# Transformer blocks on one core: the memory's keys and values projected around the attentions, and attention rows turned by halves

## The chip, the core and the metric

The kernel runs on one NeuronCore of a Trainium2 chip, as one launch. The metric is the device time of that launch in microseconds (us), as a median of several runs. TensorE (PE) multiplies, VectorE (DVE) and ScalarE (ACT) copy, split and reduce, GpSimd (POOL) does the small roots of the norms, and SyncE (SP) only issues the loads of weights. Each engine runs its own instructions in the order in which they are written. They meet through semaphores.

## What is computed

Three transformer layers on 256 rows of width 1024, in float32. The first has a masked attention of 8 heads beside a retention of 4 heads, then a cross attention of 4 heads onto 256 memory rows, then a gated MLP:

```python
h = rms_norm(x, g_pre_mix[l]);  proj = h @ w_in[l]
...
mo = merge_heads(moba_attention(mq, mk, split_heads(mv, MOBA_HEADS)))
ro = retention(rq, rk, split_heads(rv, RET_HEADS))
ro = ro * lax.rsqrt(jnp.mean(ro * ro, axis=-1, keepdims=True) + NORM_EPS)
ro = jax.nn.silu(rg) * merge_heads(ro).astype(x.dtype)
x = x + rms_norm(jnp.concatenate([mo, ro], axis=-1) @ w_out[l], g_post_mix[l])
h = rms_norm(x, g_pre_cross[l]);  mem_n = rms_norm(mem, g_mem[l])
x = x + rms_norm(cross_attention(h, mem_n, w_cq[l], w_ckv[l], w_co[l]), g_post_cross[l])
h = rms_norm(x, g_pre_ffn[l]);  gu = h @ w_gate_up[l]
x = x + rms_norm((jax.nn.silu(gu[..., :D_FF]) * gu[..., D_FF:]) @ w_down[l], g_post_ffn[l])
```

With 256 rows there is one block of keys, so `moba_attention` is a plain causal attention. The second layer has an indexed sparse attention (`dsa`) and a short convolution, the third a latent attention of 16 heads (`mla`). Each of these two ends in a squared-ReLU MLP (`mlp0`, `mlp1`).

## The kernel before

**Tiling.** The 256 rows are two tiles of 128 tokens, `t` = 0 and 1. A weight matrix comes in *units* of up to 1 MB (`SCHEDULE` lists all of them). A projection of 1024 by 1024 is four units `j` = 0 to 3 of two blocks `k` of 128 rows each, with outputs 1024 wide in two PSUM banks. Four units can be held at a time (`RING`).

**Three products.** Precision comes from splitting. ScalarE writes the rounded high part `w_hi` of a unit (`split`, L572), then VectorE the rest `w_lo` (L950, or L952 where the gain of a norm is folded in). The rows are split in the same way: TensorE turns four blocks of 128 columns into a PSUM bank (`turn`, L1463), ScalarE copies the high part `hT_hi` out (L591), VectorE subtracts it to get `hT_lo` (L967), and only then is the bank free (`tb_free`). `products` (L1398) then issues, for each `k`, high rows by `w_hi`, high rows by `w_lo`, low rows by `w_hi`, each for both banks: 12 matmuls for a unit and a token tile, 24 for a unit. Before the first of them TensorE waits for `w_low` of the unit (`split_ready`). A unit's slot is given back (`w_used`) when its last product with tile 1 is issued.

**Projections.** `project` runs all units for tile 0, then all for tile 1. Its `hooks` put other work of TensorE ahead of a given `(t, j)`. When a tile is through, ScalarE copies it out of PSUM (`group`, L631, "eviction"), and adds to `acc_copied`; TensorE waits for it before it writes those banks again.

**Attention.** For each head `hd`, TensorE makes scores (L1498), turns the probabilities of head `hd - 2` (L1506) and multiplies the values of head `hd - 3` (L1515). VectorE makes the masked maximum (L1096, or L1100 in the cross attention) and copies the turned probabilities (L1109). ScalarE makes the exponentials (L725). At the end VectorE waits for the last head, takes the reciprocal of all sums and scales the output into `h` (`normalise`, L1122 and L1124). Only then TensorE turns `h`, and the output projection follows.

**Order of the first layer.** Input projection, first attention, retention, `out`; then the memory's keys (`mem_k`), the memory's values (`mem_v`), the cross queries (`cross_q`), the cross attention, `cross_o`, and the MLP `ffn`. The memory's rows are turned into `gT_hi` and `gT_lo` near the end of the input projection. `SCHEDULE`, the loads on SyncE, and the code of ScalarE, VectorE and TensorE all carry this order, written out by hand.

**Boundaries.** After an output projection, `boundary` weighs the result by a gain (`weigh`, L1030, from PSUM into `h`), adds it to the stream `x` (`add_to_stream`, L1039), splits the next units in between, and turns the new rows. ScalarE takes the sum of squares of each tile (L645), GpSimd the root (L463, L464). An MLP that follows starts with its chunk 0. Its first hidden tile (`part`, L745 and L747 on ScalarE, `act_part`, L1134 and L1138 on VectorE) comes after `split_to(m.u0 + 3)`, the split of the fourth unit. TensorE waits for that hidden tile before it starts chunk 1, since the PSUM bank is used again.

## Time and profile before

| | us |
|---|---|
| median of 3 runs | 1106.6 |
| lowest, highest | 1105.09, 1107.01 |
| the profiled execution, its own time | 1103.71 |
| its span, first to last instruction | 1101.9 |
| TensorE busy | 1048.6 (95%) |
| VectorE busy | 656.2 (60%) |
| ScalarE busy | 563.5 (51%) |

A profile is of one execution, so durations read from it add up to its own span. The profile has a page with busy times and the costliest groups, a timeline (each instruction with its start, its duration and the idle time before it, with what ended that), the chain of work that ended last, and tables of stretches with the granted TensorE clock. Ends of matmuls are modelled: in a run of 512-wide matmuls each is drawn as 0.39 us long while the next starts 0.23 us after it, so that the drawn idle time after such a matmul is 0.16 us less than what TensorE lost.

### The profile page before, as it was taken

To read this page: it belongs to the slowest core of one execution; us is meant where nothing else is said; L and a number is where in the kernel's file an instruction comes from. 1 tells how busy PE (TensorE), PEld (TensorE's weight loads), DVE (VectorE), ACT (ScalarE), POOL (GpSimd) and SP (SyncE) were. 2 spreads that over 40 slices of the span, in tenths; PEclk is the share of its full clock that TensorE was granted. 3 is DMA by queue.
4 is the path that set the end of the run, shared out by engine and by line. 5 is a ranking of instruction groups with operands and counts; after the bars stand their busy time and mean duration, and the time that the engine had idled before them with its cause. 6 is when DMAs were issued, how large, how long until landed. Compare 5 with 4: busy or idle time off the path is not lost.

```text
span 1101.9 us, 13842 instructions
## 1 busy us (share of the span) xinstructions
PE 1048.6 (95%) x5080; PEld 872.6 (79%) x5080; DVE 656.2 (60%) x1010; ACT 563.5 (51%) x855; POOL 97.7 (9%) x127
## 2 busy tenths in 40 slices
PE   7998999999999999999989999999997999999997
PEld 6887788777888888878767788888886877888886
DVE  5567654466645655648786655555654866555553
ACT  6555554346554544744454654544454646545441
POOL 2010110001000000203540100000140001000000
PEclk9999999999999999999999999999999999999999
DMA  9642265224455455543422555554252225555521
GB/s 345 274 177 77 94 233 189 77 78 170 172 188 211 157 188 200 211 153 115 153 77 106 219 191 181 199 190 145 75 182 110 77 107 199 191 180 200 188 80 38
DMA packets 28461, 176.29 MB, mean 160 GB/s; under 512 B 3248, under 2 KB 3392, under 8 KB 9984
## 3 DMA queue, kind: packets, MB, share of 16 engines
q1 hardware_dynamic: 26784, 170.08, 42.6%
q0 software_dynamic: 1456, 5.48, 1.3%
q8 instruction: 29, 0.48, 0.2%
q10 hardware_dynamic: 176, 0.13, 0.0%
q14 instruction: 16, 0.13, 0.0%
HBM read 174.62 MB, written 1.05 MB: 159 GB/s over the span
## 4 chain that ended last, share of the span: by engine, by line
PE 84%; DVE 7%; ACT 4%; issue 2%; POOL 2%; DMA 1%; SPq 0%; DVEq 0%; ACTq 0%; POOLq 0%
PE PS L1398 74%; PE PS L1463 4%; DVE w_lo L952 2%; PE PS L1515 2%; ACT w_hi L572 2%; PE PS L1593 2%; PE PS L1498 2%; DVE work L1096 1%; POOL rstd L464 1%; POOL h L487 1%; DMA x<-in_x 1%; DVE w_lo L950 1%; PE PS L1506 1%; DVE h L1281 1%; POOL arena L480 1%
## 5 line engine op out<-in xcount | busy, mean ns | idle before, releaser
L952 DVE SCALAR_TENSOR_TENSOR w_lo<-w_raw,gcol,w_hi 128x512 fp32r<-128x512 f32 (+4 forms) x322 | 269.5, 894 | 206.0 <-ACT w_hi L572 205.4
L1398 PE MATMUL PS<-w_hi,hT_hi 128*128 128x512 f32 (+3 forms) x904 | 320.1, 395 | 17.8 <-DVE hT_lo L967 5.1
L1398 PE MATMUL PS<-w_lo,hT_hi 128*128 128x512 f32 (+3 forms) x904 | 313.2, 388 | 0.0
L1398 PE MATMUL PS<-w_hi,hT_lo 128*128 128x512 f32 (+3 forms) x904 | 313.0, 387 | 0.0
L572 ACT ACTIVATE w_hi<-w_raw,gcol 128x512 fp32r<-128x512 f32 (+4 forms) x322 | 243.4, 823 | 99.9 <-PE PS L1398 99.2
L1398 PEld LDWEIGHTS PS<-w_hi,hT_hi 128*128 128x128 f32 x904 | 168.3, 190 | 53.3 <-DVE w_lo L952 11.7
L1398 PEld LDWEIGHTS PS<-w_hi,hT_lo 128*128 128x128 f32 x904 | 170.7, 190 | 34.0
L1398 PEld LDWEIGHTS PS<-w_lo,hT_hi 128*128 128x128 f32 x904 | 170.8, 190 | 32.8
L950 DVE TENSOR_TENSOR w_lo<-w_raw,w_hi 128x2048 fp32r<-128x2048 f32 (+1 forms) x70 | 135.8, 1953 | 89.3 <-ACT w_hi L572 89.2
L572 ACT ACTIVATE w_hi<-w_raw 128x2048 fp32r<-128x2048 f32 (+1 forms) x70 | 114.8, 1645 | 102.8 <-PE PS L1398 102.8
L1398 PE MATMUL PS<-w_hi,gT_hi 128*128 128x512 f32 x408 | 126.2, 390 | 0.0
L1398 PE MATMUL PS<-w_hi,gT_lo 128*128 128x512 f32 x408 | 125.8, 390 | 0.0
L1398 PE MATMUL PS<-w_lo,gT_hi 128*128 128x512 f32 x408 | 125.7, 389 | 0.0
L1398 PEld LDWEIGHTS PS<-w_lo,gT_hi 128*128 128x128 f32 x408 | 76.6, 188 | 16.0
L1398 PEld LDWEIGHTS PS<-w_hi,gT_lo 128*128 128x128 f32 x408 | 76.5, 188 | 15.9
L463 POOL TENSOR_SCALAR msq<-ssq 128x1 f32<-128x1 f32 (+1 forms) x31 | 11.0, 354 | 872.9 <-ACT work L645 827.5
L1398 PEld LDWEIGHTS PS<-w_hi,gT_hi 128*128 128x128 f32 x408 | 76.1, 188 | 15.4
L631 ACT ACTIVATE arena<-PS,rstd 128x1024 f32<-128x1024 f32 (+1 forms) x24 | 25.0, 1043 | 60.6 <-PE PS L1398 44.7
L591 ACT ACTIVATE hT_hi<-PS 128x512 fp32r<-128x512 f32 (+1 forms) x46 | 25.2, 582 | 53.5 <-PE PS L1463 53.4
L967 DVE TENSOR_TENSOR hT_lo<-PS,hT_hi 128x512 fp32r<-128x512 f32 (+1 forms) x46 | 29.2, 668 | 30.2 <-ACT hT_hi L591 30.0
L1498 PE MATMUL PS<-arena 128*128 128x256 f32 (+1 forms) x160 | 36.4, 361 | 6.8 <-ACT arena L631 2.7
L645 ACT ACTIVATE work<-PS 128x1024 f32<-128x1024 f32 x14 | 14.4, 1028 | 51.7 <-PE PS L1398 51.7
(149 smaller groups left out, 790.5 us busy)
## 6 DMA issues: line engine op xcount, KB each, us to landing
w_raw<-in_w SPq DMA_DIRECT2D x64, 1024.0 KB, 4.8
w_raw<-in_w_gu SPq DMA_DIRECT2D x22, 1024.0 KB, 4.8
w_raw<-in_w_in SPq DMA_DIRECT2D x11, 1024.0 KB, 7.3
w_raw<-in_w_dn SPq DMA_DIRECT2D x22, 512.0 KB, 5.2
w_raw<-in_w_out SPq DMA_DIRECT2D x4, 1024.0 KB, 4.8
w_raw<-in_w_mem_k SPq DMA_DIRECT2D x4, 1024.0 KB, 4.8
w_raw<-in_w_mem_v SPq DMA_DIRECT2D x4, 1024.0 KB, 4.9
w_raw<-in_w_cq SPq DMA_DIRECT2D x4, 1024.0 KB, 5.7
```

Source lines behind the costliest of these rows:

```text
L572: ins = act.activation(w_hi[:, u % RING, k * w:(k + 1) * w], w_raw[:, u % RAW, k * w:(k + 1) * w], ACT.Copy, scale=1.0 if col is None else ...
L591: act.activation(d, PS[:, 4 + n["tb"] % 4, 0:blocks * P].rearrange("p (b m) -> p b m", m=P), ACT.Copy).then_inc(tb_high, 1)
L631: ins = act.activation(dst, src, ACT.Copy, scale=scale)
L645: act.activation(square_out if out is None else out, src, ACT.Square, scale=scale, accum_out=ssq[:, n["norm"]:n["norm"] + 1]).then_inc(ss_ ...
L950: ins = dve.tensor_tensor(lo, raw, hi, ALU.subtract)
L952: ins = dve.scalar_tensor_tensor(out=lo, in0=raw, scalar=gcol[:, col + TURNED * k:col + TURNED * k + 1], in1=hi, op0=ALU.mult, op1=ALU.sub ...
L967: dve.tensor_tensor(lo, PS[:, 4 + n["tb"] % 4, 0:blocks * P].rearrange("p (b m) -> p b m", m=P), hi.bitcast(F32), ALU.subtract).then_inc(t ...
L1398: mm = pe.matmul(bank(t, j)[:, 0:width], rows[:, kc0 + k, tok], w[:, s, at:at + width], start=begin and i == 0, stop=end and i == 2)
L1463: mm = pe.transpose(PS[0:rows, 4 + n["tb"] % 4, i * P:(i + 1) * P], src, ident[:])
L1498: mm = pe.matmul(PS[:, 4 + hd % 2, c0:c1], q, k, start=i == 0, stop=i == len(pairs) - 1)
L1515: mm = pe.matmul(out_banks(a, t)[:, hd * a.dv:(hd + 1) * a.dv], a.ET[hd % 2][:, c0 + s * P:c0 + (s + 1) * P], a.v(hd, s), start=s == 0, st ...
L1593: mm = pe.transpose(m.turn_bank[t][:, b * P:(b + 1) * P], hidden[:, t, b * P:(b + 1) * P], ident[:])
```

## The change

In the first layer `mem_k` is projected straight after the input projection, unit by unit for both tiles, with the scores of attention heads 0 and 1 ahead of its last unit's two halves. `mem_v` is projected behind `cross_q` in the same way, with the scores of the first two cross heads inside it. The loads and splits follow that order. `products` goes through a unit in three passes (high by high, low rows by `w_hi`, high rows by `w_lo`) and waits for `w_high` first and for `w_low` only ahead of the third. The output of the cross attention and of `mla` is scaled, turned and split in two halves of 512 columns, the first half while the last heads still run; `cross_o` and `odd_out` start on it. `weigh` writes into `work`. The retention's scaling and gate are one instruction a head instead of two a tile. At the start of each MLP the first hidden tile comes ahead of the split of the fourth unit.

```diff
-            ("out", plain_units(4)), ("mem_k", gained("mem", 4, 2, 2048)), ("mem_v", gained("mem", 4, 2, 2048)),
-            ("cross_q", gained("pre_cross", 4, 2, 2048)), ("cross_o", plain_units(4)),
+            ("mem_k", gained("mem", 4, 2, 2048)), ("out", plain_units(4)), ("cross_q", gained("pre_cross", 4, 2, 2048)),
+            ("mem_v", gained("mem", 4, 2, 2048)), ("cross_o", plain_units(4)),
...
+        cross.score_bank, cross.prob_bank = 6, 4
...
 # ScalarE, boundary
                 if not hidden_next:
                     high_rows(hT_hi, 1)
-                split_to(e + 3)
+                    split_to(e + 3)
...
 # ScalarE, mlp (VectorE the same with act_part)
-                split_to(m.u0 + 3)
                 part(0, tiles=[0])
+                split_to(m.u0 + 3)
+                part(0, tiles=[1])
                 split_to(m.u0 + 4)
-                part(0, tiles=[1])
...
 # ScalarE, memory keys and first attention
+            n["used"] += 4
+            split_to(n["used"] + 1)
+            attention(moba, [0])
+            split_to(n["used"] + 2)
+            evict(0, rows2(k_tok), mem_rows)
+            attention(moba, [1])
+            evict(1, rows2(k_tok), mem_rows)
+            attention(moba, range(2, moba.H), False)
+            split_to(n["used"] + 3)
...
 # VectorE, the same place
+            split_to(n["used"] + 1)
+            attention(moba, [0])
+            split_to(n["used"] + 2)
+            attention(moba, range(1, moba.H + 2), False)
...
 # VectorE, attention
+                    elif rows is not None:
+                        normalise_half(a, rows, hd - a.H, 0)
                     if hd >= 2:
                         copy_turned(hd - 2)
+            def normalise_half(a, dst, t, half):
+                heads = slice(half * a.H // 2, (half + 1) * a.H // 2)
+                if t == 0:
+                    dve.wait_ge(a.summed, heads.stop)
+                    steps.link(dve.reciprocal(a.sums[:, heads, :], a.sums[:, heads, :]))
...
 # TensorE, products
-                for k in range(kcs):
-                    begin, end = first and k == 0, last and k == kcs - 1
-                    for i, (rows, w) in enumerate(((hi, w_hi), (hi, w_lo), (lo, w_hi))):
+                if fresh:
+                    high_ready(u, it)
+                for i, (rows, w) in enumerate(((hi, w_hi), (lo, w_hi), (hi, w_lo))):
+                    if fresh and i == 2:
+                        split_ready(u, it)
+                    for k in range(kcs):
...
+            def out_project(tile, **more):
+                at = n["tb"] - 2
+                project(4, 2, wide, rows=lambda t, half: at + 2 * half + t, second=lambda: pe.wait_ge(h_ready, n["h"] + 1),
+                        hooks={(0, 1): lambda: turn_half(tile, 512), (1, 2): tile0}, **more)
...
 # TensorE, the first layer
-            copied()
-            turned(6)
-            attention(moba)
+            by_unit = [(t, j) for j in range(4) for t in range(TT)]
+            project(4, 2, wide, gT_hi, gT_lo, copies=2, rows=n["tb"] - 6, order=by_unit,
+                    hooks={(0, 3): moba_scores, (1, 3): lambda: attention(moba, [1])})
+            attention(moba, [2])
+            copied()
+            attention(moba, range(3, moba.H + 3))
...
-            project(4, 2, wide, gT_hi, gT_lo, copies=2, hooks={(1, 0): tile1})
-            project(4, 2, wide, gT_hi, gT_lo, copies=2, hooks={(1, 1): lambda: turn_rows(k_tok, False)})
-            project(4, 2, wide, copies=2)
-            copied()
-            turn_rows(q_tok, False)
-            turned(4)
-            attention(cross)
-            turn_rows(h)
-            rows = n["tb"] - 4
-            project(4, 2, wide, rows=rows, hooks={(1, 2): tile0})
-            mlp(ffn, within=half_of(0, 0))
+            project(4, 2, wide, copies=2, rows=n["tb"] - 2, hooks={(0, 3): tile1})
+            project(4, 2, wide, gT_hi, gT_lo, copies=2, order=by_unit,
+                    hooks={(0, 1): query_rows, (0, 3): cross_scores, (1, 3): lambda: attention(cross, [1])})
+            attention(cross, [2])
+            copied()
+            attention(cross, range(3, cross.H + 3), h)
+            out_project(h)
+            mlp(ffn, between={(2, 0): half_of(0, 0)})
```

**VectorE around the first two heads of the first attention.** Before, the two maxima of a head (the rows with `causal`) follow each other head by head:

```order
L950 TENSOR_TENSOR w_lo<-w_raw,w_hi 128x2048 x2
L1096 ISA work,attention_max<-PS,causal 128x128
L1096 ISA attention_max 128x1
L1096 ISA work,attention_max<-PS,causal 128x256
L1096 ISA attention_max 128x1
L1103 TENSOR_SCALAR attention_bias<-attention_max 128x2
L1096 ISA work,attention_max<-PS,causal 128x128
```

After (L981 is the old L950, L1127 the old L1096, L1134 the old L1103):

```order
L981 TENSOR_TENSOR w_lo<-w_raw,w_hi 128x2048 x2
L1127 ISA work,attention_max<-PS,causal 128x128
L1127 ISA attention_max 128x1
L1127 ISA work,attention_max<-PS,causal 128x256
L1127 ISA attention_max 128x1
L1134 TENSOR_SCALAR attention_bias<-attention_max 128x2
L981 TENSOR_TENSOR w_lo<-w_raw,w_hi 128x2048
L1127 ISA work,attention_max<-PS,causal 128x128
```

The third unit of `out` is now split between head 0 and head 1.

**VectorE from the second tile's rows to the first hidden tiles of `ffn`.** Before:

```order
L1039 SCALAR_TENSOR_TENSOR x<-h,rstd,x 128x512 x2
L967 TENSOR_TENSOR hT_lo<-PS,hT_hi 128x4x128 x2
L952 SCALAR_TENSOR_TENSOR w_lo<-w_raw,gcol,w_hi 128x512 x8
L1134 SCALAR_TENSOR_TENSOR arena<-PS,rstd,arena 128x256
L950 TENSOR_TENSOR w_lo<-w_raw,w_hi 128x1024
```

After:

```order
L1070 SCALAR_TENSOR_TENSOR x<-work,rstd,x 128x512 x2
L998 TENSOR_TENSOR hT_lo<-PS,hT_hi 128x4x128 x2
L983 SCALAR_TENSOR_TENSOR w_lo<-w_raw,gcol,w_hi 128x512 x4
L1186 SCALAR_TENSOR_TENSOR arena<-PS,rstd,arena 128x256
L983 SCALAR_TENSOR_TENSOR w_lo<-w_raw,gcol,w_hi 128x512 x4
```

The first hidden tile (L1134, now L1186) stands between the third and the fourth unit instead of behind both.

**VectorE in the last heads of the cross attention, after.** Here L1140 is the copy of the turned probabilities (before L1109), and L1157 and L1158 are the reciprocal and the scaling of one half:

```order
L1140 COPY work<-PS 128x512
L1157 RECIPROCAL attention_sum<-attention_sum 128x4
L1158 TENSOR_TENSOR h<-PS,attention_sum 128x512
L1140 COPY work<-PS 128x512
L1158 TENSOR_TENSOR h<-PS,attention_sum 128x512
```

Before, the reciprocal and two scalings of 128x1024 stood behind all four copies. Now the first half's reciprocal stands ahead of the copy for head 2.

## Rows read from the trace of the kernel before

**Rows 1.** Page, part 1: busy us (share of the span), instructions.

```profile
PE 1048.6 (95%) x5080; PEld 872.6 (79%) x5080; DVE 656.2 (60%) x1010; ACT 563.5 (51%) x855; POOL 97.7 (9%) x127
```

**Rows 2.** Chain that ended last: start us, us, what (engine, tile, line, instructions).

```profile
88.37 0.99 ACT work L725 x4
...
92.27 0.33 PE PS L1506 x3
92.59 0.62 PE PS L1515 x6
93.21 0.71 PE PS L1498 x4
...
97.27 0.29 DVE work L1096
...
98.03 0.57 DVE work L1109
...
101.39 1.36 PE PS L1532 x8
...
213.64 1.73 PE PS L1498 x8
...
367.20 16.38 PE PS L1398 x72
```

**Rows 3.** Timeline where the first attention starts: start, us, what, [idle before, releaser].

```profile
84.74 3.81 PE L1498 MATMUL PS<-arena 128*128 128x128 f32 x12 [2.70 <-ACT arena L631]
...
83.55 1.13 ACT L631 ACTIVATE arena<-PS,rstd 128x1024 f32<-128x1024 f32 x1
```

**Rows 4.** Chain from the retention's norm to the third unit of `out`.

```profile
112.21 1.30 DVE h L1243 x2
...
116.07 1.91 ACT w_hi L572
...
118.00 2.30 DVE w_lo L950
...
120.35 8.50 PE PS L1398 x36
```

**Rows 5.** Timeline of TensorE: cross queries turned, cross attention's rows turned.

```profile
204.36 1.97 PE L1463 MATMUL PS<-ident,arena 128*128 128x128 f32 x16 [1.21 <-ACT arena L631]
...
225.15 2.22 PE L1463 MATMUL PS<-ident,h 128*128 128x128 f32 x16 [1.56 <-DVE h L1124]
```

**Rows 6.** Timeline where `ffn` starts its chunk 1, all engines.

```profile
257.50 0.94 POOL L464 TENSOR_TENSOR rstd<-msq,neg_half 128x1 f32<-128x1 f32 x1
...
260.74 1.28 ACT L745 ACT_TABLE_LOAD   x1
262.04 0.47 ACT L745 ACTIVATE arena<-PS,rstd 128x256 f32<-128x256 f32 x1
...
260.76 2.74 DVE L952 SCALAR_TENSOR_TENSOR w_lo<-w_raw,gcol,w_hi 128x512 fp32r<-128x512 f32 x4 [1.40 <-ACT w_hi L572]
263.41 0.48 DVE L1134 SCALAR_TENSOR_TENSOR arena<-PS,rstd,arena 128x256 f32<-128x256 f32 x1
...
264.04 0.47 PE L1398 MATMUL PS<-w_hi,hT_hi 128*128 128x512 f32 x1 [1.86 <-DVE arena L1134]
```

**Rows 7.** Timeline of TensorE where `mlp0` starts its chunk 1.

```profile
620.05 0.52 PE L1398 MATMUL PS<-w_hi,hT_hi 128*128 128x512 f32 x1 [2.06 <-DVE arena L1138]
```

**Rows 8.** Stretches: length, busy us (instructions), granted clock as a share, DMA.

```profile
265.30:268.80 3.50, 3.50 (x10) 2.76 (x9) 1.25 (x2) 0.00 (x0) 0.00 (x0) 0.51 0.92 320
...
470.00:473.50 3.50, 3.50 (x12) 2.92 (x12) 3.42 (x8) 2.74 (x5) 0.00 (x0) 0.52 0.90 332
```

**Rows 9.** Timeline of TensorE at a unit of the second layer's `conv` projection.

```profile
533.89 0.74 PE L1398 MATMUL PS<-w_hi,hT_hi 128*128 128x512 f32 x2 [1.04 <-DVE w_lo L952]
```

**Rows 10.** Timeline at `ukv` in the third layer: VectorE, then TensorE.

```profile
828.00 4.87 DVE L952 SCALAR_TENSOR_TENSOR w_lo<-w_raw,gcol,w_hi 128x1024 fp32r<-128x1024 f32 x4 [1.18 <-ACT w_hi L572]
...
835.06 1.20 PE L1463 MATMUL PS<-ident,h 128*96 128x128 f32 x8 [0.19 <-DVE h L1017]
```

277 lines of the change are left out of this document (160 added, 117 removed).

## The prediction

> **What bounds the kernel now.** I read the page's busy times first. TensorE is busy 95% of the span, VectorE 60% [rows 1]. The chain of work then shows long pieces of products that follow without a gap, 72 in 16.38 us, or 0.2275 us each [rows 2]. The change leaves the number and shape of the products as they are, so nearly all of the 1102 us stays. What can go is time in which TensorE waits, and time at the lower clock. So I went through TensorE's timeline for rows with idle time, and for each I ask whether the change puts work there and what comes late next. To a drawn idle time after products 0.16 us is added, since a product is drawn longer (0.39) than its distance to the next. Positive numbers below are time saved.
>
> **Start of the first attention.** The products of the input projection could have gone on at 84.74 - 2.70 - 0.16 = 81.88 [rows 3]; the attention is through at 101.39 [rows 2]: 19.5 us. A head costs TensorE 0.33 + 0.62 + 0.71 = 1.66 us [rows 2], eight cost 13.3. So 6.2 us are waits for evictions and first exponentials, and slow clock. Now the keys' four units stand there, 24 x 0.2275 = 5.46 us each. Count from their start. The scores of head 0 come after three units (16.4 to 17.1), half a unit follows to 19.8, scores of head 1 to 20.5, half a unit to 23.3, then scores and turning, 1.0 us, to 24.3. There TensorE waits for the second eviction of the keys. Who leads to it: maximum of head 0 (0.8, from 97.27 to 98.03) to 17.9, exponentials (1.0) to 18.9 [rows 2], ScalarE's split of the third `out` unit (1.9) to 20.8, VectorE's part of it (2.3) to 23.1 [rows 4], maximum and exponentials of head 1 to 24.9, eviction (1.1) [rows 3] to 26.0. That is 1.7 us, and with semaphores about 2.1 us late. Behind the waiting TensorE instruction stand all values of the attention. The gain is 6.2 - 2.1 = 4.1; I take 3.8, for a slower end of the last heads. Ends: 6.2 if nothing is late, 2 if the new wait also brings the low clock.
>
> **`out`.** The gated rows depend on VectorE's scaling, which starts at 112.21, while the chain goes on over a split of the third unit (1.91, 2.30) to 120.35 [rows 4]. Now 16 turnings of the keys (16 x 0.11 = 1.75 us, the same as elsewhere before) fill part of that wait, and that unit has been split earlier. Eight 128x128 instructions replace four of 128x512 on VectorE; the nearest row is the 128x128 maximum of 0.29 us [rows 2], so the first tile costs 1.2 instead of 2.0. But VectorE now has its split of the last unit (2.3) directly ahead. I take 1.3, ends 0.5 and 2.3.
>
> **Start of the cross attention.** From 204.36 - 1.21 - 0.16 = 203.0 to 225.15 - 1.56 - 0.15 = 223.4 [rows 5] are 20.4 us. The work is 16 turnings (1.75), 4 x 1.73 for scores, 4 x 1.73 for values [rows 2] and four turnings of a head at 0.44 (four of 0.11): 17.4. The 3.0 us of waits now lie behind the values' units. Here the second eviction comes in time: from the scores of head 0, the path is 1.7 + 0.9 + 1.0 + 1.9 + 2.3 + 0.9 + 1.0 + 1.1 = 10.8 us, and TensorE reaches it after 1.7 + 2.7 + 1.7 + 2.7 + 1.7 + 0.4 = 10.9. Gain 3.0, ends 2 and 3.0.
>
> **Its end.** From 223.4 to 227.4 [rows 5] TensorE does 1.75 us of turnings, 2.2 are lost. By halves the reciprocal and first scaling fall into the last heads. But VectorE waits for the values of head 1 ahead of its copy for head 2, and TensorE's values of head 2 are queued behind that copy: 0.2 + 0.65 + 0.7 for the three, less 0.44 of turning, gives 1.2 us of new wait. Gain 1.0, ends 0 and 2.2. In `mla`, where the same two turnings cost the same 2.2, the first eight heads are long done when VectorE asks, so only some 0.6 is left: 1.6.
>
> **MLP starts.** `ffn` stands still for 1.86 + 0.16 = 2.0 us for its first hidden tile [rows 6]; the two others for 2.2 each, one row for both [rows 7]. The root is there at 257.50 + 0.94 = 258.44. Table load 1.28 and activation 0.47 then give about 260.0, VectorE's 0.48 gives 260.5, ahead of TensorE's 262.0. What is late next is the second hidden tile, behind the fourth unit's splits: ScalarE 2.6 us to 262.5, VectorE 2.74 to 265.3, then 0.48 [rows 6], while TensorE wants it at 262.0 + 12 x 0.2275 = 264.8. So 1.0 is left of 2.0. In the other two there is no table load, and 0.3 is left of 2.2. Gain 1.0 + 1.9 + 1.9 = 4.8, ends 3 and 6.4.
>
> **The clock.** Right behind the wait in `ffn`, TensorE is granted 0.51, its 1.2 GHz level, for about 3.4 us [rows 8], which costs products 1.7 us. The same stands behind both other MLP starts, and in each case TensorE had stood idle for 2.0 us or more. One fall, at 470, came without idle time [rows 8], while it issued 80-column products, and stays. With waits of 1.0 us and less I take these three falls away: 3 x 1.7 = 5.1, ends 0 and 5.1.
>
> **The passes.** A wait for `w_lo` now comes 8 products (1.8 us) later in a unit with two blocks. At `conv` this takes the 1.04 + 0.16 of the row [rows 9], and another 0.8 in its next unit, down to 0.2: 1.8. Unit waits at `uq` (0.7) and twice at `out` projections (0.4 here, the other is counted) follow the pattern: 1.1. At `ukv` it saves nothing: VectorE's splits run from 828.00 to 832.9, its rotation after them, and TensorE must wait for that until 835.06 [rows 10]. It will get there 1.8 us earlier and stand idle for 3.6 us, so the low clock falls on work behind it instead of before: -1.6. The added waits and the pace of products: the loads of stationary rows are one for each product, as before (5080 and 5080, [rows 1]), so I take 0, ends 0 and -25 (a rival).
>
> **Sum.** 3.8 + 1.3 + 3.0 + 1.0 + 1.6 + 4.8 + 5.1 + 1.8 + 1.1 - 1.6 = 21.9. The profiled execution took 1103.7 and would take 1081.8; the median of the runs lies 2.9 higher, 1106.6 - 21.9 = 1084.7.
>
> **A rule against it.** ScalarE's change of function costs 1.28 us in the row, and the activation starts 0.02 us after it (260.74 + 1.28, next 262.04) [rows 6]. The Trainium skill, "ScalarE: Activation LUTs", section "What ACT_TABLE_LOAD costs", says 1.28 us and a drain of 1.38 beside it, 2.66 in all, for every switch. The trace doesn't agree, as no such drain is drawn between these two rows. By that rule the load in `ffn` would lead to a second hidden tile 1.4 us later.
>
> **Rivals.** (a) *The low clock stays, or comes back elsewhere* (at the keys' new wait of 2 us, at the MLP starts): the moved waits add up to enough idle time for it. For it speaks the fall at 470 without idle; against it that TensorE passed waits of 1.7 us at 225.15 at full clock. Price 5.1 + 1.3: 1091. (b) *The drain*: if a table load holds ScalarE 1.4 us longer, `ffn` keeps a wait of 2.4 and its low clock: 1.4 + 1.7, 1088. (c) *New waits eat the moved starts*: the order on ScalarE and VectorE between head 0 and head 1 delays the attentions by more than I count, both starts and both ends give nothing (9.4): 1094. (d) *Slower than before*: products in the new order have another pace. The third pass uses `w_lo` against rows last loaded a pass ago, and each unit has a second wait. There are some 3,700 products of 512 columns. From 6 ns more on each (0.2275 to 0.2335) it costs 22 us and eats the whole gain; 10 ns give 1122. Against it: pairs of products on the same rows (wide outputs) and single ones (512) run at the same 0.2275, waits that are met cost nothing in the loops. (e) *The change doesn't do what it says*, since the halves of `mem_k` are bound by the loads: its units' slots come free 5.5 us apart, SyncE is far ahead; nothing speaks for it, time as (c).
>
> **Chances.** Forecast 0.62; (a) 0.15, (b) 0.04, (c) and (e) 0.14, (d) 0.05, of which 0.03 slower. The forecast's own spread, from the ends above, is 1078 to 1090. The range takes in (a), (b) and most of (c): 1077 to 1095. A measurement can tell 0.2%, about 2 us. Faster 0.95, within it 0.02, slower 0.03.
>
> **What would show it.** Right: products at 0.2275 us; about 2 us of idle before the values of head 0; no idle row ahead of the second cross head; at most 1.0 us at the three MLP starts and full clock behind them; 3.6 us of idle at `ukv`. Wrong: a pace above 0.23, a wait of over 1 us at the first product of `cross_q` (rows of the stream not ready), low-clock stretches at as many places as before, or VectorE behind in the keys' units.

## The result, and the profile after

The changed kernel takes 1089.9 us (median of 4, 1089.14 to 1090.19), the kernel before beside it 1106.3 us (1105.09 to 1107.01): ratio 0.9852, 95% interval 0.9841 to 0.9864. That is 16.4 us less, where 21.9 were forecast. The profiled execution after took 1089.14 us with a span of 1087.3. TensorE's busy time hardly moved, as should be, since its instructions are the same [rows 1]:

```profile
span 1087.3 us, 13860 instructions
## 1 busy us (share of the span) xinstructions
PE 1044.9 (96%) x5080; PEld 872.4 (80%) x5080; DVE 655.1 (60%) x1020; ACT 564.1 (52%) x855; POOL 99.8 (9%) x127
```

**Where the time went.** Both kernels have 5080 products, so the k-th product can be looked up in each trace. The table gives the time between the starts of two of them, the first being product 0. Between 351 and 1060 the change moves products, so of the kernel before and `b_mlp` on the one side and all others on the other only the sum of the two rows can be compared there (150.3 us before, 142.6 after). Elsewhere the same product is at most a dozen places further on. The kernels of the experiments are explained below.

| TensorE's products, stage | before | b_mlp | after | after_again | a_front | a_bias2 | best | best_front |
|---|---|---|---|---|---|---|---|---|
| 0 to 351, input projection | 75.5 | 75.3 | 76.3 | 76.6 | 76.3 | 77.0 | 76.0 | 76.4 |
| to 560, first attention (before: to the middle of `out`) | 41.6 | 42.5 | 39.1 | 40.8 | 39.1 | 40.8 | 37.8 | 37.8 |
| to 1060, the rest up to `cross_o` | 108.7 | 108.7 | 103.5 | 103.5 | 103.5 | 103.5 | 101.4 | 101.4 |
| to 1216, rest of `cross_o`, start of `ffn` | 37.4 | 35.0 | 35.0 | 35.0 | 35.1 | 35.1 | 35.0 | 35.0 |
| to 2430 | 262.4 | 262.4 | 262.4 | 264.0 | 262.4 | 264.0 | 262.4 | 262.4 |
| to 2541, end of `conv` | 24.9 | 24.9 | 23.1 | 23.1 | 24.9 | 23.1 | 23.1 | 24.9 |
| to 2700, `dsa` attention, start of `even_out` | 35.1 | 35.1 | **38.4** | 35.8 | 35.0 | 33.5 | 32.8 | 31.2 |
| to 3740, rest of `even_out`, `mlp0`, `down`, `uq`'s first tile | 222.1 | 218.7 | 218.0 | 217.9 | 218.6 | 217.9 | 217.9 | 218.7 |
| to 3815, rest of `uq` | 13.6 | 13.6 | 14.0 | 13.9 | 13.6 | 14.0 | 14.9 | 13.6 |
| to 3900, `ukv` | 21.5 | 21.4 | 22.8 | 22.8 | 21.4 | 23.9 | 19.5 | 19.8 |
| 4000 to 5079, `mla`'s end, `odd_out`, `mlp1` | 228.3 | 226.0 | 224.0 | 224.0 | 227.5 | 224.0 | 223.8 | 227.3 |

(3900 to 4000 is 17.9 in all.) From before to after that is a gain of 14.6 us of the 1089.0 between the first and the last product. Of the stages that were forecast faster the rest of `uq` is 0.4 slower, and 3.4 us are lost in the row of `dsa`, which the prediction did not mention. One thing was plain only with several executions: the stretches at the 1.2 GHz level don't lie at the same products each time. The changed kernel's own second trace (after_again) has one in the first attention, where the first has none, and less of them in `dsa`. A difference of 1.7 us in one stage of one trace can be this alone, and in `dsa` the changed kernel's two traces differ by 2.6.

**What came as forecast.** The keys' new wait, with the split ahead of head 1's maximum, as the path in the prediction has it (1.75 us idle, 2.0 between starts):

```profile
103.53 2.29 DVE L981 TENSOR_TENSOR w_lo<-w_raw,w_hi 128x2048 fp32r<-128x2048 f32 x1 [2.86 <-ACT w_hi L572]
...
107.51 1.09 ACT L631 ACTIVATE h<-PS,rstd 128x1024 f32<-128x1024 f32 x1
...
106.42 0.49 PE L1580 MATMUL PS<-ident,work 128*128 128x128 f32 x3
108.65 0.92 PE L1572 MATMUL PS<-arena 128*128 128x128 f32 x4 [1.75 <-ACT h L631]
```

The cross attention starts without a wait [rows 5] and has the forecast one at its end (first row below, where L1140 stands behind one half's scaling). The second hidden tile is what is late in `ffn` (1.07 + 0.16 us for 2.0 [rows 6]), and the two other starts have 0.21 + 0.16 for 2.2 each, one row for both [rows 7]:

```profile
215.16 1.13 PE L1589 MATMUL PS<-arena,work 128*128 128x256 f32 x4 [1.16 <-DVE work L1140]
...
259.04 1.20 PE L1468 MATMUL PS<-w_hi,hT_hi 128*128 128x512 f32 x4 [1.07 <-DVE arena L1186]
...
613.08 1.20 PE L1468 MATMUL PS<-w_hi,hT_hi 128*128 128x512 f32 x4 [0.21 <-DVE arena L1190]
...
528.21 1.21 PE L1468 MATMUL PS<-w_lo,hT_hi 128*128 128x512 f32 x4 [0.17 <-DVE w_lo L983]
...
823.51 3.32 PE L1537 MATMUL PS<-ident,h 128*96 128x128 f32 x16 [3.33 <-DVE h L1048]
```

The last two rows are `conv`'s remaining wait for `w_lo` (1.04 before [rows 9]; 0.2 forecast) and the idle time at `ukv` (3.3 idle, 3.7 from one start to the next; 3.6 forecast).

The clock, in stretches (columns: from:to, length, busy and instructions of each engine, granted clock, DMA share, GB/s): full speed behind the starts of `mlp0` and `mlp1`, still half speed at 461, as at 470 before [rows 8], at `ukv`, and now around `dsa`:

```profile
461.20:464.60 3.40, 3.40 (x9) 2.64 (x9) 3.37 (x8) 2.76 (x5) 0.00 (x0) 0.51 0.93 354
549.90:553.30 3.40, 2.90 (x8) 2.02 (x8) 1.56 (x6) 0.89 (x1) 2.87 (x2) 0.50 0.54 227
556.80:563.60 6.80, 6.67 (x26) 5.70 (x27) 5.74 (x18) 3.29 (x15) 6.16 (x3) 0.51 0.00 0
823.00:826.40 3.40, 2.89 (x14) 2.76 (x15) 1.14 (x3) 0.66 (x2) 0.00 (x0) 0.51 0.76 306
612.00:620.00 8.00, 7.79 (x38) 6.19 (x37) 6.62 (x6) 5.91 (x8) 0.00 (x0) 1.00 0.92 335
912.00:920.00 8.00, 7.79 (x39) 6.22 (x38) 6.49 (x7) 5.91 (x9) 0.00 (x0) 1.00 0.79 294
```

**What did not.** At `out`, GpSimd's mean of squares for 8 columns took 2.17 us; before it took 0.20:

```profile
129.04 2.28 DVE L981 TENSOR_TENSOR w_lo<-w_raw,w_hi 128x2048 fp32r<-128x2048 f32 x1
133.15 2.16 DVE L1304 SCALAR_TENSOR_TENSOR arena<-PS,rstd,arena 128x128 f32<-128x128 f32 x8 [1.82 <-POOL rstd L464]
...
129.21 2.17 POOL L463 TENSOR_SCALAR msq<-ssq 128x8 f32<-128x8 f32 x1 [62.90 <-DVE ssq L1296]
131.46 1.65 POOL L464 TENSOR_TENSOR rstd<-msq,neg_half 128x8 f32<-128x8 f32 x1
```

The same instruction in the kernel before:

```profile
110.25 0.20 POOL L463 TENSOR_SCALAR msq<-ssq 128x8 f32<-128x8 f32 x1 [44.68 <-DVE ssq L1236]
```

The prediction saw VectorE's split of the last unit ahead of the scaling, but counted it on VectorE alone. It also stands in GpSimd's way: it ends at 131.32, GpSimd's instruction at 131.38.

At `dsa`, TensorE waits 2.39 us for VectorE's product L1386 (1.06 before), then for the biases of the heads:

```profile
548.20 1.26 PE L1537 MATMUL PS<-ident,arena 128*128 128x128 f32 x8 [2.39 <-DVE arena L1386]
...
554.31 0.92 PE L1572 MATMUL PS<-arena 128*128 128x128 f32 x4 [1.08 <-DVE attention_bias L1134]
...
545.25 2.29 DVE L981 TENSOR_TENSOR w_lo<-w_raw,w_hi 128x2048 fp32r<-128x2048 f32 x1
547.46 1.29 DVE L1386 TENSOR_TENSOR arena<-arena 128x512 f32<-128x512 f32 x2
...
552.66 1.59 DVE L1134 TENSOR_SCALAR attention_bias<-attention_max 128x2 f32<-128x2 f32 x1
...
554.83 1.85 DVE L1134 TENSOR_SCALAR attention_bias<-attention_max 128x2 f32<-128x2 f32 x1
...
565.21 0.17 DVE L1134 TENSOR_SCALAR attention_bias<-attention_max 128x2 f32<-128x2 f32 x1
...
552.33 1.89 POOL L502 TENSOR_TENSOR arena<-arena,conv_w 128x1020 f32<-128x1020 f32 x1
554.30 2.35 POOL L503 TENSOR_TENSOR arena<-arena 128x1020 f32<-128x1020 f32 x1
```

Two things are to be seen. First, VectorE's chain (splits, top-k, split, copies, split, product) bounds this place. Its top-k part began 9.34 us earlier than before (530.95 for 540.29), while TensorE came 11.2 us earlier, so that of the 1.8 us gained in `conv` 1.3 are idle time at this product. Second, a bias of 2 columns takes 0.17 us when GpSimd is idle and up to 1.85 while it convolves, and it ends with GpSimd's instruction (552.66 + 1.59 = 554.25, GpSimd 554.22; 554.83 + 1.85 = 556.68, GpSimd 556.65). In the kernel before the same rows stand, but the first bias met only the last 0.3 us of a GpSimd instruction (until 562.08):

```profile
561.76 0.34 DVE L1103 TENSOR_SCALAR attention_bias<-attention_max 128x2 f32<-128x2 f32 x1
...
562.68 1.39 DVE L1103 TENSOR_SCALAR attention_bias<-attention_max 128x2 f32<-128x2 f32 x1
...
560.18 1.90 POOL L500 TENSOR_TENSOR arena<-arena,conv_w 128x1024 f32<-128x1024 f32 x1 [20.12 <-DVE arena L985]
```

So the cost was there before. What the change altered is how the engines meet. Summed over the whole row of `dsa`, though, TensorE's drawn idle time grew only from 7.2 to 7.6 us, since longer waits at some products made others shorter. The rest of the 3.4 us is products at half speed: none before, 10.2 us of the row after, 3.4 us in after_again (where 0.8 us are lost).

### The profile page after: what moved, and what is told of

The parts are those of the page before. It is cut to its first block, busy times and chain, and to the rows that moved or that the text cites. A ratio compares the mean times of both kernels' runs of the same rounds, so it can differ in the third digit from the quotient of the medians.

```text
span 1087.3 us, 13860 instructions
## 1 busy us (share of the span) xinstructions
PE 1044.9 (96%) x5080; PEld 872.4 (80%) x5080; DVE 655.1 (60%) x1020; ACT 564.1 (52%) x855; POOL 99.8 (9%) x127
## 3 DMA queue, kind: packets, MB, share of 16 engines
HBM read 174.62 MB, written 1.05 MB: 162 GB/s over the span
## 4 chain that ended last, share of the span: by engine, by line
PE 82%; DVE 9%; ACT 3%; issue 3%; POOL 2%; DMA 1%; SPq 0%; DVEq 0%; ACTq 0%; POOLq 0%
PE PS L1468 71%; PE PS L1537 3%; DVE w_lo L983 3%; PE PS L1589 2%; PE PS L1572 2%; ACT w_hi L572 2%; PE PS L1679 2%; DVE w_lo L981 1%; DMA x<-in_x 1%; DVE work L1127 1%; POOL h L487 1%; PE PS L1580 1%; DVE h L1347 1%; POOL arena L480 1%; ACT work L653 0%
## 5 line engine op out<-in xcount | busy, mean ns | idle before, releaser
L1468 PE MATMUL PS<-w_hi,hT_hi 128*128 128x512 f32 (+3 forms) x904 | 246.4, 393 | 7.8 <-DVE hT_lo L998 3.0
L1468 PE MATMUL PS<-w_hi,hT_lo 128*128 128x512 f32 (+3 forms) x904 | 240.2, 386 | 0.0
L1468 PE MATMUL PS<-w_lo,hT_hi 128*128 128x512 f32 (+3 forms) x904 | 238.9, 385 | 0.9 <-DVE w_lo L983 0.8
L1468 PEld LDWEIGHTS PS<-w_lo,hT_hi 128*128 128x128 f32 x904 | 167.5, 188 | 35.9 <-DVE w_lo L983 2.4
L1468 PEld LDWEIGHTS PS<-w_hi,hT_hi 128*128 128x128 f32 x904 | 164.0, 189 | 40.1 <-issue 3.8
L1468 PEld LDWEIGHTS PS<-w_hi,hT_lo 128*128 128x128 f32 x904 | 168.1, 189 | 33.2
L981 DVE TENSOR_TENSOR w_lo<-w_raw,w_hi 128x2048 fp32r<-128x2048 f32 (+1 forms) x70 | 135.7, 1954 | 83.7 <-ACT w_hi L572 83.6
L1468 PE MATMUL PS<-w_hi,gT_hi 128*128 128x512 f32 x408 | 113.9, 392 | 0.0
L1468 PE MATMUL PS<-w_lo,gT_hi 128*128 128x512 f32 x408 | 112.9, 390 | 0.0
L1468 PE MATMUL PS<-w_hi,gT_lo 128*128 128x512 f32 x408 | 112.7, 389 | 0.0
L1468 PEld LDWEIGHTS PS<-w_hi,gT_lo 128*128 128x128 f32 x408 | 76.6, 188 | 16.0
L631 ACT ACTIVATE arena<-PS,rstd 128x1024 f32<-128x1024 f32 (+1 forms) x22 | 22.8, 1036 | 44.7 <-PE PS L1468 30.7
L733 ACT ACTIVATE work<-work,attention_bias 128x128 f32<-128x128 f32 x64 | 28.5, 446 | 31.2 <-DVE attention_bias L1134 31.2
```

What stands on the lines that cost most here:

```text
L631: ins = act.activation(dst, src, ACT.Copy, scale=scale)
L733: ins = act.activation(a.E[hd % 3][:, c0:c1], src, ACT.Exp, bias=a.nb[:, hd, t:t + 1], scale=a.scale, accum_out=a.sums[:, hd, t:t + 1])
L981: ins = dve.tensor_tensor(lo, raw, hi, ALU.subtract)
L1468: mm = pe.matmul(bank(t, j)[:, 0:width], rows[:, kc0 + k, tok], w[:, s, at:at + width], start=begin and i == 0, stop=end and i == 2)
```

## The experiments

My theory of the shortfall was then: GpSimd blocked at `out` (1 to 2 us), VectorE's chain, the blocked biases and the clock at `dsa` (3.4), and small terms. Rivals were the new order of the passes, the keys' wait and the end of cross. Each run is timed beside the kernel before (medians of 1105.15 to 1106.15 us in four groups).

**The MLP starts alone** (b_mlp, the kernel before with this part only; here ScalarE's part of the edit; VectorE's moves the same steps):

```diff
                 if not hidden_next:
                     high_rows(hT_hi, 1)
-                split_to(e + 3)
+                    split_to(e + 3)
...
-                split_to(m.u0 + 3)
                 part(0, tiles=[0])
+                split_to(m.u0 + 3)
+                part(0, tiles=[1])
                 split_to(m.u0 + 4)
-                part(0, tiles=[1])
```

> The kernel before with one part of the change alone: at the three MLP starts ScalarE and VectorE serve the first hidden tile between the splits of the third and fourth unit, and ScalarE's boundary split stands where the change has it. Theory (the prediction's own terms): waits 1.0 + 1.9 + 1.9 less and three stretches at the 1.2 GHz level gone, 5.1, together 9.9 us, so about 1096.4 us; full clock behind all three MLP starts, and nothing moved elsewhere. Rival: the clock's gain needs the other parts too (other idle times go, or the low clock moves elsewhere): then only the waits, 4.8 us, 1101.5.

Measured 1098.9 us (ratio 0.9942, 0.9926 to 0.9958), its executions in two groups, 1096.2 to 1097.5 (granted clock 0.992 and 0.993) and 1100.3 to 1100.5 (0.986). The median lies between the two cases, and the lower group at the theory's 1096.4; the trace is of that group, so what the upper one has more is not shown. At the places themselves the theory's 9.9 is met to 0.6: 2.4 at `ffn`, 3.5 at `mlp0` and 3.4 at `mlp1` (between products 4280 and 4340), and the clock behind them is full:

```profile
265.00:270.00 5.00, 3.94 (x20) 2.89 (x19) 3.96 (x5) 0.79 (x1) 0.00 (x0) 1.00 0.62 229
620.00:626.00 6.00, 6.00 (x33) 5.01 (x32) 4.83 (x4) 3.91 (x7) 0.00 (x0) 1.00 0.91 360
878.80:882.10 3.30, 3.20 (x15) 3.20 (x16) 2.43 (x4) 1.54 (x3) 0.00 (x0) 0.50 0.00 0
```

But a stretch of half speed now stands at `odd_out` (last row), where the kernel before has idle time at full clock. It costs 1.1 us (products 4120 to 4200). The one near the first attention has moved from 84 to 117.6. Part of what an MLP start gives back in clock is taken elsewhere.

**The late wait for `w_lo`** (a_front, the changed kernel without it):

```diff
                 if fresh:
-                    high_ready(u, it)
+                    split_ready(u, it)
                 for i, (rows, w) in enumerate(((hi, w_hi), (lo, w_hi), (hi, w_lo))):
-                    if fresh and i == 2:
-                        split_ready(u, it)
```

> The changed kernel with the wait for w_lo put back ahead of each unit's first product (the order of the three passes stays). The prediction's ledger says it is worth 1.8 at conv and 1.1 elsewhere, less 1.6 lost at ukv: without it 1089.9 + 1.3 = 1091.2 us. Theory from the trace of after: the conv gain is given back a few us later, because VectorE's own chain (splits, top-k, split, copies, split, product) bounds the start of the dsa attention: TensorE's wait of 2.39 us there falls to about 1.0, and the 3.3 us at ukv to about 1.6 us. Then 1088 to 1090 us, so that the later wait is worth nothing here or costs a little.

Measured 1090.4 us (0.9869, 0.9851 to 0.9886): between the two, and the intervals of this and the changed kernel overlap. The table tells more than the sum. `conv` loses 1.8, and `dsa` gets 3.4 back (0.8 against after_again), with TensorE's wait down to 1.06 as the theory has it. `uq` gets 0.4 back and loses 0.7 in its first tile. `ukv` gets 1.35 back, but not as the theory has it: the wait of 3.33 is down to 1.45, yet one of 2.82 for `w_lo` stands ahead of it (817.81), and the idle time of the stage is 0.3 longer; what is gained is the half-speed stretch, which is gone. What neither case had is the last stage, which loses 3.4:

```profile
548.75 1.26 PE L1535 MATMUL PS<-ident,arena 128*128 128x128 f32 x8 [1.06 <-DVE arena L1386]
...
879.78 1.16 PE L1466 MATMUL PS<-w_hi,hT_hi 128*128 128x512 f32 x4 [2.23 <-DVE w_lo L981]
...
877.34 4.49 DVE L981 TENSOR_TENSOR w_lo<-w_raw,w_hi 128x2048 fp32r<-128x2048 f32 x2 [1.00 <-ACT w_hi L572]
```

By halves, `odd_out`'s products start before VectorE has split their unit. In the changed kernel the split starts as late (879.93), but is wanted only in the third pass and costs 0.18 us. So the late wait carries the halves of `mla`.

The totals show what the two waits trade. TensorE's drawn idle time is 34.1 us here and 29.7 in the changed kernel, but the half-speed stretches between the first and the last product sum to 6.8 us here and to 17.1 there. The late wait saves idle time and pays for most of it in clock.

**GpSimd at `out`** (a_pool):

```diff
-            split_to(n["used"] + 3)
             dve.wait_ge(ret_rstd, 1)
             dve.wait_ge(gate_ready, 1)
...
             low_banks(2, half_rows(4))
+            split_to(n["used"] + 3)
             boundary(0, 4, hidden_next=False)
```

> The changed kernel with VectorE's split of out's last unit moved behind the gating and the low halves. Theory: GpSimd's tensor_scalar of 8 columns took 2.17 us at 129.21 because it stood locked out while VectorE's split ran (129.04 to 131.32); with VectorE idle it took 0.20 in the kernel before. Expected 0.2 us again, gating 2.0 us earlier, TensorE's two waits ahead of out (1.34 and 1.73 between starts) 2 us shorter in sum, 1088 us. Rival: the 2.17 us is how GpSimd's span happens to be drawn, or the gating waits for something else (ScalarE's reading of the gate): then the row stays near 2, or the gating stays at 133.15 and the time at 1089.9.

Measured 1086.7 us (0.9840, 0.9823 to 0.9856). The theory holds; the lock is seen by its absence:

```profile
128.67 0.20 POOL L463 TENSOR_SCALAR msq<-ssq 128x8 f32<-128x8 f32 x1 [62.90 <-DVE ssq L1296]
...
130.63 2.16 DVE L1303 SCALAR_TENSOR_TENSOR arena<-PS,rstd,arena 128x128 f32<-128x128 f32 x8 [2.06 <-POOL rstd L464]
...
136.36 1.17 PE L1468 MATMUL PS<-w_hi,hT_hi 128*128 128x512 f32 x4 [1.62 <-DVE hT_lo L998]
```

The gating starts 2.5 us earlier, of which 0.5 comes from ahead of it, as the input projection is shorter in this trace. Products 560 to 1060 take 102.3 for 103.5: 1.2 us, not 2, since TensorE now waits (1.62) for VectorE's low part of the last turned rows, where it had two waits of 1.07 and 1.46. The medians differ by 3.2, more than this place gives; this trace has no half-speed stretch near 461, which is worth 1.6 us, and its executions spread from 1086.3 to 1089.5.

**VectorE's chain at `dsa`** (a_dsa: `after_group(4, lambda: plain_banks(4, turned_qk3), 1)` with 0 for 1, so that one split comes in the middle of the heads):

> The changed kernel with VectorE's split of one even_out unit moved from ahead of the two products for the convolution rows to the middle of the dsa attention. Theory: VectorE's chain bounds the start of this attention, so TensorE's wait of 2.39 us at 548.20 falls by about 2.2, and with less idle time the stretch at the low clock behind it may go as well: gain 1.5 to 4 us, 1086 to 1088.4, less what the 2.3 us cost in the middle of the heads (up to 1). Rival: TensorE waits there for ScalarE's evictions or the turned rows, so that the wait stays: 1089.9, or the split in the middle of the heads costs 2.3 us: 1090.

Measured 1092.1 us (0.9879, 0.9863 to 0.9895), slower than the changed kernel by 2.2, where 1.5 to 4 us less were expected. The first step goes the expected way, but less far: the wait at L1386 falls from 2.39 to 1.05, by 1.34 for 2.2. The gain is lost behind it, and more: the stage takes 40.8 us. The rival (1090) was right in kind and too low in price.

```profile
546.67 1.26 PE L1537 MATMUL PS<-ident,arena 128*128 128x128 f32 x8 [1.05 <-DVE arena L1386]
...
564.03 1.54 PE L1589 MATMUL PS<-arena,work 128*128 128x64 f32 x6 [4.49 <-DVE work L1140]
...
557.48 3.81 DVE L981 TENSOR_TENSOR w_lo<-w_raw,w_hi 128x2048 fp32r<-128x2048 f32 x1
...
561.88 1.64 DVE L1134 TENSOR_SCALAR attention_bias<-attention_max 128x2 f32<-128x2 f32 x1
...
557.16 1.98 POOL L503 TENSOR_TENSOR arena<-arena 128x1016 f32<-128x1016 f32 x1
559.22 4.27 POOL L504 TENSOR_TENSOR arena<-arena 128x1024 f32<-128x1024 f32 x1
```

This is the lock from both sides. The split (2.29 alone) starts inside a GpSimd instruction, waits for its end (559.14) and ends 2.15 us later. GpSimd's last product (2.36 elsewhere) waits for the split in turn, and the next bias waits for that product.

**The bias without the lock** (a_bias2: in `dsa`, VectorE counts up `maxed` when the maxima are there, and ScalarE scales them):

```diff
+                    if a is dsa:
+                        act.activation(a.nb[:, hd, :], a.mx[:, hd, :], ACT.Copy, scale=-a.scale).then_inc(biased, 1)
+                        act.wait_ge(biased, hd + 1)
...
-                    dve.tensor_scalar(a.nb[:, hd, :], a.mx[:, hd, :], -a.scale, None, ALU.mult).then_inc(a.maxed, 1)
+                    if a is dsa:
+                        dve.sem_inc(a.maxed, 1)
+                    else:
+                        dve.tensor_scalar(a.nb[:, hd, :], a.mx[:, hd, :], -a.scale, None, ALU.mult).then_inc(a.maxed, 1)
```

> The changed kernel, but in the dsa attention ScalarE instead of VectorE scales the row maxima to the bias (2 columns a head), so that VectorE has only instructions that read PSUM while GpSimd convolves. Theory: VectorE's bias instruction took 1.59, 1.85, 1.38 and 1.02 us there, each ending within 0.05 us of the end of a GpSimd instruction of the convolution, against 0.17 us behind it: it is locked out. TensorE's scores wait for it. Expected: no such instruction, heads 0 to 4 at 1.7 us instead of 2.1 to 2.4, one or both stretches at the 1.2 GHz level (549.92 and 556.75) shorter or gone, 1 to 4 us gained: 1086 to 1089. Rival: VectorE's maxima take the lock's place (they read a mask from SBUF too and grow from 0.29 and 0.42), or ScalarE's extra instruction a head makes ScalarE the bound: 1089.9 or more.

Measured 1087.9 us (0.9831, 0.9811 to 0.9850). The stage takes 33.5 us, 5.0 less than in the changed kernel's first trace and 2.4 less than in its second. The second is the fair comparison, since it has as much low clock in this stage (3.4 us). VectorE's maxima keep 0.29 and 0.42 us, so the rival is out, and from head 4 on the heads follow at 1.65 us. The first bias had a price of its own: ScalarE's table load now stood behind the first bias, in the path.

```profile
556.38 0.20 ACT L730 ACTIVATE attention_bias<-attention_max 128x2 f32<-128x2 f32 x1 [2.81 <-DVEq L1139]
556.60 1.28 ACT L737 ACT_TABLE_LOAD   x1
```

**The keys' wait, two ways.** a_keys2 moves the split of the third `out` unit behind head 2, on ScalarE and VectorE:

```diff
             attention(moba, [0])
-            split_to(n["used"] + 2)
             evict(0, rows2(k_tok), mem_rows)
             attention(moba, [1])
             evict(1, rows2(k_tok), mem_rows)
-            attention(moba, range(2, moba.H), False)
+            attention(moba, [2], False)
+            split_to(n["used"] + 2)
+            attention(moba, range(3, moba.H), False)
```

> The changed kernel with the split of the third out unit moved on ScalarE and VectorE behind the work for head 2 of the first attention. Theory: that split (1.9 on ScalarE, 2.3 on VectorE) stands in the chain that leads to the second eviction of the keys and so to TensorE's wait of 2.0 us at 108.65; without it the wait is gone: 1088 us. Rival: the wait returns behind it, as the split is then late for out's third unit or lengthens a later head: 1089.9.

Measured 1095.7 us (0.9904, 0.9888 to 0.9920), 6 us slower than the changed kernel: the wait at the keys is gone (0.22), and one of 3.85 us stands two heads on, behind the same split, with 6.8 us at half speed from 111.2 on. The first attention takes 44.2 us for 39.1, 5.1 of the 5.8 us between the medians. The rival was right in kind and far too low in price.

```profile
106.02 0.92 PE L1573 MATMUL PS<-arena 128*128 128x128 f32 x4 [0.22 <-ACT h L631]
...
112.78 1.54 PE L1590 MATMUL PS<-arena,work 128*128 128x64 f32 x6 [3.85 <-DVE work L1141]
```

a_evict leaves the split and puts the second eviction ahead of head 1's exponentials, on ScalarE alone:

```diff
-            attention(moba, [1])
             evict(1, rows2(k_tok), mem_rows)
+            attention(moba, [1])
```

> The changed kernel with two steps of ScalarE exchanged in the first attention: the second eviction of the keys ahead of head 1's exponentials. The last product of the keys started at 105.55 in the trace of after, ScalarE was idle from 104.5 to 106.61, and evicted at 107.51, behind the exponentials of head 1, which wait for VectorE's split and maximum. Theory: the eviction starts at about 106.0, TensorE's wait at 108.65 falls from 1.75 to 0.3, exponentials of head 1 end at 108.0 instead of 107.5, ahead of their turning: 1.3 us gained, 1088.3. Rival: TensorE waits there for VectorE (maximum or copy of head 1), so the wait stays; or, as with the split moved behind head 2, it only comes later: 1089.5 or more.

Measured 1088.9 us (0.9845, 0.9831 to 0.9858), and the stage takes 37.8 for 39.1: 1.35 us, as forecast. The eviction starts at 105.61, in time that ScalarE had idle. The median shows 1.0 of it. The trace has a half-speed stretch from 136.3, in a wait of 1.46 us that the changed kernel has too, and loses 1.5 us behind it.

```profile
105.61 1.11 ACT L631 ACTIVATE h<-PS,rstd 128x1024 f32<-128x1024 f32 x1 [1.46 <-PE PS L1468]
...
106.78 0.92 PE L1572 MATMUL PS<-arena 128*128 128x128 f32 x4 [0.22 <-ACT h L631]
```

**The end of cross** (a_cross2: in each step `copy_turned` ahead of `normalise_half`):

> The changed kernel with VectorE's copy of the turned probabilities ahead of the first half of the scaling in every step of the last two. Theory: the wait of 1.2 us between the turning of the last head and the values at 215.16 is this order's cost: it goes, and the second tile's halves come 0.7 later at most, so 0.5 to 1.2 us gained at the end of cross and up to 0.6 in mla: 1089.0. Rival: the first rows are what TensorE waits for next, so that the same time is lost there: 1089.9.

Measured 1089.5 us (0.9841, 0.9820 to 0.9861), within what the changed kernel's executions spread. In the trace the wait at 215.16 is gone and products 920 to 1060 take 27.9 for 28.8 us, the last stage 0.15 less. 1 us is below what the medians resolve here, so this rests on the trace, and on best, which has the same 27.9. This trace, too, has a half-speed stretch at product 648 (from 138.8) that the changed kernel's has not, and loses 1.5 us there.

**The rotation at `ukv`** (a_ukv2):

```diff
-            after_group(3, lambda: queries_turned(0), 1)
+            after_group(3, lambda: queries_turned(0), 0)
             rotate(heads_of(stages[1], 96), 64, 16, cos4, sin4).then_inc(h_ready, 1)
+            split_to(n["used"] + 1)
```

> The changed kernel with VectorE's rotation of the second queries ahead of its split of the second ukv unit. Theory: the rotation ends 2 us earlier (about 821.5), TensorE's wait at 823.51 falls from 3.3 to 1.5 us, and the low clock behind it (822.99 to 826.40) may go: 1.8 to 3.5 us gained, 1086.4 to 1088.1, with a wait for w_lo in the second unit of at most 0.5. Rival: the rotation waits for ScalarE's reading of the queries (818.39 to 819.28 and 820.21 to 821.5), so that only 0.5 us is gained and the split is late for its unit: 1090.

Measured 1088.1 us (0.9846, 0.9831 to 0.9862). In the trace TensorE's wait is 1.41 us and the clock behind it full; the stage takes 19.5 for 22.8, 3.3 us, as the theory has it. The medians show 1.8 of it, within their spread.

`ukv` takes 22.7 to 24.2 us in the other kernels that leave its order alone and keep the late wait.

```profile
820.42 2.47 DVE L983 SCALAR_TENSOR_TENSOR w_lo<-w_raw,gcol,w_hi 128x1024 fp32r<-128x1024 f32 x2
820.56 1.95 PE L1538 MATMUL PS<-ident,h 128*96 128x128 f32 x16 [1.41 <-DVE h L1048]
```

**All that helped, together, and the changed kernel once more.**

> The changed kernel itself, beside the two others of this call on one chip, to see how much its executions spread and where its low-clock stretches lie in another one. Theory: 1089 to 1090 us in the median; the same idle times ahead of TensorE at the same products; the stretches at the 1.2 GHz level may lie at other products than in the first trace, since the granted clock of the executions of one kernel spread too (0.981 to 0.989 for the kernel before).

> The changed kernel with five edits: out's last split behind the gating, the copy ahead of the half scaling, the rotation ahead of ukv's second split, the second eviction of the keys ahead of head 1's exponentials, and dsa's bias on ScalarE, now with its function table loaded ahead of the first scores (ScalarE's load of 1.28 us stood at 556.60 behind the first bias). By the stretches between the same products of the single edits: 1.2 + 1.0 + 3.3 + 1.3 + 5.0 and up to 1 for the table load, 12 to 13 us, so 1077 us. Rival: the single gains share the low-clock stretches (which return elsewhere when one place is mended): then only their idle times count, 1.2 + 1.0 + 1.8 + 1.3 + 2.5 = 7.8, 1082 us.

after_again: 1089.9 us (1087.4 to 1093.0; 0.9852, 0.9832 to 0.9872). best: 1076.9 us (1076.1 to 1077.4; 0.9734, 0.9720 to 0.9747), 13 us less than the changed kernel beside it. The sum of the stages was right, 1077, and the rival's 1082 was not: most of the single gains do not share the same clock. In the traces TensorE's idle time falls from 29.7 to 21.6 us and the half-speed stretches from 17.1 to 10.2. One stretch did come at a new place, at 795.2 in `uq`, and costs 0.9. In `dsa` the table load is off the path, ahead of the first maximum:

```profile
545.70 1.28 ACT L726 ACT_TABLE_LOAD   x1
547.00 0.20 ACT L726 ACTIVATE attention_bias<-ident 128x2 f32<-128x2 f32 x1
```

**The late wait once more**, in best (best_front, same diff as a_front):

> The five edits of best, with the wait for w_lo put back ahead of each unit's first product, as in the changed kernel's variant a_front. There the trace showed what the later wait carries: at odd_out TensorE waited 2.23 us for w_lo (879.78), which VectorE splits behind its scaling and low halves (877.34 to 881.8); in the changed kernel the same split starts as late, at 879.93, and costs 0.18. Theory: the wait at odd_out (2.2) comes back, with 1.2 us more if the low clock falls on it, conv gives 0.5 net (1.8, of which 1.3 is idle time at dsa's start again), uq and even_out 1.0: 1076.9 + 3.7 to 4.9 = 1080.6 to 1081.8 us. Rival (the prediction's ledger, in which the later wait is worth 1.8 + 1.1 and the attention's halves need nothing of it): 1079.8; or nothing, as between the changed kernel and a_front, 1077.4.

Measured 1080.6 us (1079.3 to 1081.2; 0.9767, 0.9754 to 0.9780), 3.7 more than best, at the lower end of the theory. By the median alone the rival's 1079.8 is not excluded; the stages tell them apart. `conv` loses 1.8 and the row of `dsa` gives 1.65 back, so the late wait is worth 0.15 there, and 0.7 at `uq`'s first tile. At `odd_out`, where the rival had nothing, it is worth 3.5, of which 2.23 us is a wait and the rest the clock. Against it stands best's stretch in `uq`, which is not there (1.3 us less).

## Why the prediction was right, and where its terms were off

The forecast was 1084.7 with 1077 to 1095, the time is 1089.9. On the profiled executions the sum was 21.9 and the difference 14.6 (1103.7 to 1089.1). By its own terms:

| term | forecast | measured | from |
|---|---|---|---|
| start of the first attention | 3.8 | 3.6 | 19.3 us to the retention's start before; 37.5 less 96 products of 0.2275, so 15.7, after |
| start and end of cross | 4.0 | 3.9 | the same way: 24.3 us before; 39.5 less 84 products, 20.4, after |
| `out` | 1.3 | 0.2 | retention to the end of `out`: 33.8 us before; 35.3 less 16 turnings of 0.11, 33.6, after |
| `ffn` with its clock | 2.7 | 2.4 | table |
| `mlp0`, `mlp1` with their clock | 7.2 | 6.9 | 3.5 by b_mlp and 3.4 between products 4280 and 4340 |
| `conv` | 1.8 | 1.8 | table |
| `uq`, `even_out` | 1.1 | 0.7 | 0.7 at `uq`'s third unit, 0.4 at `even_out` (2686 to 2698), -0.4 later in `uq` |
| `ukv` | -1.6 | -1.2 | table |
| end of `mla` | 1.6 | 0.8 | last stage 4.2, less 3.4 |
| `dsa` | not in it | -3.8 | table, without the 0.4 of `even_out` |
| input projection | not in it | -0.7 | table; the other kernels spread by 2.0 |

- **Right in mechanism and size:** the interleaving of the keys with its new wait, the cross attention's two terms, the three MLP starts, `conv` by itself and the loss at `ukv`. (Two workings are slightly off: 0.2 + 0.65 + 0.7 less 0.44 is 1.1, not 1.2, and 258.44 + 1.28 + 0.47 is 260.2, not 260.0. Neither moves a term by more than 0.2.) The pace of products stayed at 0.2275 us, so rival (d) did not come about. Nor did (b): behind `ffn`'s table load (251.60, 1.28) the next activation starts at 252.90, and the wait there is 1.07 with full clock behind it. Rivals (c) and (e) did not either: the moved starts kept their gains.
- **`out`, mis-sized, 0.2 for 1.3.** The step "VectorE now has its split of the last unit (2.3) directly ahead" was right but only half the cost: the same split blocks GpSimd, which computes what the scaling waits for. That cost 2.0 us in the row, and 1.2 of it reached TensorE (a_pool), so that the term without it would be 1.4.
- **`conv`, right in place, void in sum.** The prediction took "this takes the 1.04 + 0.16 of the row" as a gain of the kernel. It did not ask what is late next, as it did elsewhere. VectorE's chain to `dsa` is. With the late wait `dsa`'s row is longer by 3.4 us (after against a_front), 0.8 (after_again against a_front) and 1.65 (best against best_front). Little of that is idle time in sum (0.4, 0.3 and 0.6); the rest is clock. A half-speed stretch begins between products 2545 and 2553 in all ten traces with the late wait, and in none of the four without it (before, b_mlp, a_front, best_front). The wait at 2542 just ahead is 2.4 us in nine of the ten and 1.05 to 1.06 in the four; but a_dsa, with 1.05, has the stretch too, so the length of that wait alone does not decide it.
- **The late wait's real worth stands under another term.** "End of `mla`" counted on the halves alone. Without the late wait, TensorE would have stood 2.23 us at `odd_out` and lost 3.4 to 3.5 (a_front, best_front).
- **The clock.** "I take these three falls away" was right for these places. But the sum took no stretch as coming elsewhere, and they do: b_mlp has one at `odd_out`, the changed kernel 10.2 us in `dsa`. Between the first and the last product the kernel before has 20.5 us at half speed, and both traces of the changed kernel have 17.1, so in sum only one fall of 3.4 us is gone, at most 1.7 us of gain. As a sum for the whole kernel the 5.1 us of clock did not hold, though each of its three places did what was forecast; what came back stands under `dsa` in the table. This is rival (a), which had 0.15 and 1091, and it holds a good part of the truth. Most of the gain is idle time: 40.2 us before, 29.7 after. I can't say which product will meet a stretch.

The 0.4 lost in `uq` follows `conv`'s pattern: TensorE comes earlier by the late wait and then stands 0.23 us ahead of product 3788 for rows that VectorE rotates (812.18, <-DVE work L1048), where before and in a_front it does not wait.

On the traces the sum was 7.3 us too hopeful, a third of it: 3.8 at `dsa`, 1.1 at `out`, 0.8 at the end of `mla`, 0.7 in the input projection, the rest small. The forecast's own spread (1078 to 1090) only just holds the 1089.9; that it lies well inside the range is due to the room left there for the rivals.

Open: why the input projection is 0.7 slower, and what decides at which products the low clock falls.

## What to carry to other kernels

A wait taken away is a gain only as far as the next engine is early: for each place, compare how much earlier the engine that releases it now starts, not only TensorE. When an instruction is moved to stand "beside" a path, look at what the third engine does there: a split of 2.3 us on VectorE moved beside a 0.2 us instruction of GpSimd costs the path 2 us. And a table of stages between the same products tells apart gains of 1 us that medians, spread by the clock, can't, if the half-speed time of each stage is read beside it: without that, one trace overstated the gain in `dsa` twofold (5.0 for 2.4).
